# A language-model block chain on one core: RWKV outputs split one round later, two output units projected inside the last round

## The reference

```python
def _rwkv7_scan(r, w, k, v, a, b):
...
    def step(S, inp):
        r_t, w_t, k_t, v_t, a_t, b_t = inp
        sa = jnp.einsum('bhij,bhj->bhi', S, a_t)
        S = (S * w_t[:, :, None, :] + sa[..., None] * b_t[:, :, None, :] + v_t[..., None] * k_t[:, :, None, :])
        y = jnp.einsum('bhij,bhj->bhi', S, r_t)
        return S, y
...
    g = jax.nn.sigmoid(xg @ g1) @ g2
...
    y = _rwkv7_scan(r_h, decay.reshape(B, T, H, N), k_h, v_h, -kk, kk * a_h)
    mu = jnp.mean(y, axis=-1, keepdims=True)
    var = jnp.mean(jnp.square(y - mu), axis=-1, keepdims=True)
    y = (y - mu) * lax.rsqrt(var + GN_EPS)
    y = y * gn_w.reshape(H, N).astype(f32) + gn_b.reshape(H, N).astype(f32)
    y = y + jnp.sum(r_h * k_h * r_k.astype(f32), axis=-1, keepdims=True) * v_h
    y = y.reshape(B, T, D).astype(x.dtype)
    return (y * g) @ w_o
```

## Time and profile before

| | |
|---|---|
| median of 3 runs (lowest to highest) | 2088.23 us (2085.95 to 2088.8) |
| profiled execution: span from first to last instruction | 2084.5 us, 3.7 us under the median |
| profiled execution: time of its own beside the span | not listed apart from the three runs |
| TensorE busy, mean granted clock | 1981.5 us (95%), 0.963 |
| VectorE, ScalarE, GpSimd busy | 1061.3, 778.6, 252.0 us |
| RWKV rounds j = 0 to 7 | from about 862 to 1098 us |
| units 0 and 1 of the output projection | 1099.45 to 1112.36 us |

### The profile page before, as it was taken

How to read it: one execution, slowest core, us unless ns; L and a number is a source line. 1 busy time by engine, 2 the same in 40 slices (tenths; PEclk the granted TensorE clock), 3 DMA queues, 4 the chain that set the end, 5 groups by cost and what they waited for, 6 DMA issues and landing times.

```text
span 2084.5 us, 35297 instructions
## 1 busy us (share of the span) xinstructions
PE 1981.5 (95%) x14503; PEld 1583.9 (76%) x14503; DVE 1061.3 (51%) x1567; ACT 778.6 (37%) x1242; POOL 252.0 (12%) x282
## 2 busy tenths in 40 slices
PE   6999899999999999899979999999989999999997
PEld 5767678888885677777767788888867878888886
DVE  6776775555325654678653644442255564444223
ACT  4333433333222345667534333232245343323221
POOL 1100000000014000322211211110100021111110
PEclk8998999999999999899999999999999999999997
DMA  8544323333332232000003133333222223333321
GB/s 307 162 132 122 91 71 100 91 101 103 111 90 63 61 91 75 6 10 9 5 27 89 53 96 95 100 114 97 82 61 82 81 71 100 92 101 99 111 83 41
DMA packets 311057, 181.09 MB, mean 87 GB/s; under 512 B 16381, under 2 KB 303763, under 8 KB 310932
## 3 DMA queue, kind: packets, MB, share of 16 engines
q1 hardware_dynamic: 305506, 162.29, 26.2%
q0 software_dynamic: 4608, 16.78, 2.5%
q10 hardware_dynamic: 818, 0.21, 0.0%
HBM read 177.16 MB, written 2.10 MB: 86 GB/s over the span
## 4 chain that ended last, share of the span: by engine, by line
PE 85%; DVE 8%; issue 3%; ACT 3%; ACTq 1%; POOL 0%; DVEq 0%; POOLq 0%
PE bank L258 22%; PE bank L260 22%; PE bank L259 22%; PE bank L2207 4%; DVE x L1399 1%; PE bank L2704 1%; PE bank L2698 1%; PE bank L1256 1%; ACT whi L236 1%; PE bank L2805 1%; PE bank L562 1%; PE bank L1258 1%; PE bank L1257 1%; PE bank L1997 1%; DVE wlo L243 1%
## 5 line engine op out<-in xcount | busy, mean ns | idle before, releaser
L243 DVE TENSOR_TENSOR wlo<-raw,whi 128x1024 fp32r<-128x1024 f32 (+1 forms) x254 | 331.0, 1304 | 669.9 <-ACT whi L236 669.8
L236 ACT ACTIVATE whi<-raw 128x1024 fp32r<-128x1024 f32 (+1 forms) x254 | 284.1, 1119 | 669.0 <-PE bank L260 663.7
L258 PE MATMUL bank<-fh_hi,whi 128*128 128x512 f32 x991 | 387.7, 391 | 0.9 <-DVE fh_lo L483 0.5
L259 PE MATMUL bank<-fh_lo,whi 128*128 128x512 f32 x991 | 386.3, 390 | 0.0
L260 PE MATMUL bank<-fh_hi,wlo 128*128 128x512 f32 x991 | 386.2, 390 | 0.0
L258 PEld LDWEIGHTS bank<-fh_hi,whi 128*128 128x128 f32 x991 | 186.4, 188 | 42.3 <-DVE fh_lo L483 1.8
L259 PEld LDWEIGHTS bank<-fh_lo,whi 128*128 128x128 f32 x991 | 186.4, 188 | 39.2 <-issue 0.5
L260 PEld LDWEIGHTS bank<-fh_hi,wlo 128*128 128x128 f32 x991 | 186.4, 188 | 38.6
L258 PE MATMUL bank<-f_hi,whi 128*128 128x512 f32 x528 | 205.7, 390 | 0.0
L260 PE MATMUL bank<-f_hi,wlo 128*128 128x512 f32 x528 | 205.4, 389 | 0.0
L259 PE MATMUL bank<-f_lo,whi 128*128 128x512 f32 x528 | 205.4, 389 | 0.0
(11 more groups left out here) (469 smaller groups left out, 3232.8 us busy)
## 6 DMA issues: line engine op xcount, KB each, us to landing
raw<-in_w_up_dram SPq DMA_DIRECT2D x44, 512.0 KB, 3.7
raw<-in_ffn_w_gate_dram SPq DMA_DIRECT2D x44, 512.0 KB, 3.7
raw<-in_ffn_w_up_dram SPq DMA_DIRECT2D x44, 512.0 KB, 3.7
raw<-in_ffn_w_down_dram SPq DMA_DIRECT2D x32, 704.0 KB, 4.3
late<-in_ada_w_dram POOLq DMA_DIRECT2D x32, 512.0 KB, 4.2
raw<-in_rwkv_w_rkv_dram SPq DMA_DIRECT2D x24, 512.0 KB, 3.4
raw<-in_w_down_dram SPq DMA_DIRECT2D x16, 704.0 KB, 4.2
early<-in_ada_w_dram SPq DMA_DIRECT2D x16, 512.0 KB, 14.4
```

What stands on the lines that cost most here:

```text
L236: act.activation(halves_of(at)[0][:, 0:kts * P], raw_unit(at, kts), ACT.Copy).then_inc(hi_ready, 1)
L243: dve.tensor_tensor(lo[:, 0:kts * P], raw_unit(at, kts), hi[:, 0:kts * P].bitcast(F32), ALU.subtract)\
L258: pe.matmul(dst, hi, rhs_hi(k), start=first and k == 0, stop=False)
L259: pe.matmul(dst, hi, rhs_lo(k), start=False, stop=False)
```

## The change

- The splits: in round j (1 to 7) ScalarE splits y of tile j - 1 behind its copy of G, and VectorE makes the lower half behind state 3. `ys_hi` now lies on the memory of the keys (bonus) and `ys_lo` on that of the values, whose tile j - 1 nobody reads any more. After the rounds only tile 7 is split.
- The last round of TensorE is written out (`pe_last_round`): between the steps of the run it makes the products of output units 0 and 1 with tiles 0 to 6, 14 of their 16 products. `Project.pe` only adds tile 7 to both.
- The gate of round 7 goes into bank 4 (RUN_BANK[0]) in two halves, the first behind state 2, the second behind the last output; VectorE's last multiplication waits for a semaphore of its own.
- `o_tm` is placed over memory that the rounds no longer need by then, and the lower halves of the FFN's held weights lie in the last tiles of `f_lo`, since `f_hi`'s tiles now overlap `ys_hi`.

```diff
+                if held_apart:
+                    held[4:] = [self.f_lo[:, n:n + 2, :].rearrange("p a n -> p (a n)") for n in range(KF - 8, KF, 2)]
...
+    with ExitStack() as part:
+        sbs(part, "y_all", [P, KD, T])
+        ys_hi = sbs(part, "ys_hi", [P, KD, T], F32R)
+        ys_lo = sbs(part, "ys_lo", [P, KD, T], F32R)
     rkv = sbs(tm, "rkv", [P, 3 * KD, T])
+    with ExitStack() as part:
+        o_tm = sbs(part, "o_tm", [P, KD, T])
...
+    def gate_bank(j):
+        return POST_BANK if j < KD - 1 else RUN_BANK[0]
...
+    def act_split_y(act, j):
+        DVEc.wait(act, j, "y")
+        act.activation(ys_hi[:, j, :], rkv[:, j, :], ACT.Copy).then_inc(ys_hi_ready, 1)
...
                 act_gt(act, j)
+                if j:
+                    act_split_y(act, j - 1)
...
     def dve_post_gate(dve, j):
-        PEc.wait(dve, j, "g")
+        if j < KD - 1:
+            PEc.wait(dve, j, "g")
+        else:
+            dve.wait_ge(last_gate, 1)
         DVEc.wait(dve, j, "yb")
-        DVEc.done(dve.tensor_tensor(r_k_v(j)[0], y_sb[:, :], bank[POST_BANK][:, :], ALU.mult), "y")
+        DVEc.done(dve.tensor_tensor(r_k_v(j)[0], y_sb[:, :], bank[gate_bank(j)][:, :], ALU.mult), "y")
+    def dve_split_y(dve, j):
+        dve.wait_ge(ys_hi_ready, j + 1)
+        dve.tensor_tensor(ys_lo[:, j, :], rkv[:, j, :], ys_hi[:, j, :].bitcast(F32), ALU.subtract)\
+           .then_inc(ys_ready, 1)
...
                 dve_state(dve, j, 3)
+                if j:
+                    dve_split_y(dve, j - 1)
...
+    def pe_last_gate(pe, part):
+        b = bank[gate_bank(KD - 1)][:, :]
+        if part == 0:
+            wait(pe, lg_landed, KD * 32)
+            ACTr.wait(pe, KD - 1, "gt0")
+            DVEr.wait(pe, KD - 1, "hp1")
+            pe.matmul(b, lg[:, 0, :], g_hid[:, :], start=True, stop=False)
+        else:
+            pe.matmul(b, lg[0:G_REST, 1, :], g_hid2[:, :], start=False, stop=True).then_inc(last_gate, 1)
+    def pe_last_round(pe):
+        j = KD - 1
+        def project(o, *ks):
+            for k in ks:
+                out_tm.pe_early(pe, o, k)
+        pe_xau(pe, j)
+        project(0, 0, 1)
+        pe_state_parts(pe, j)
+        pe_rh(pe, j, None)
+        project(0, 2)
+        pe_state(pe, j, 1)
+        pe_state(pe, j, 2)
+        pe_last_gate(pe, 0)
+        pe_state(pe, j, 3)
+        pe_local(pe, j)
+        pe_state(pe, j, 4)
+        project(0, 3)
+        pe_state(pe, j, 5)
+        project(0, 4)
+        pe_state(pe, j, 6)
+        for c in (6, 1, 3, 5, 4, 2):
+            pe_y(pe, j, c)
+        pe_y(pe, j, 7)
+        pe_last_gate(pe, 1)
+        project(0, 5)
+        pe_post_var(pe, j, None)
+        project(1, 0, 1)
+        pe_post_spread(pe, j)
+        project(1, 2, 3, 4, 5)
+        project(0, 6)
+        project(1, 6)
...
+            if j == KD - 1:
+                pe_last_round(pe)
+                return
...
+        def pe_early(self, pe, o, k):
+            self.y_split(pe, k)
+            unit_products(pe, self.at0.plus(o), KD, bank[o][:, :], lambda k: self.hi[:, k, :],
+                          lambda k: self.lo[:, k, :], True, True, ks=[k])
...
-            wait(pe, o_ready.sem, self.o0)
-            two_units(pe, [self.at0.plus(o) for o in range(2)], KD, [bank[o][:, :] for o in range(2)], hi, lo,
-                      lambda k: self.y_split(pe, k))
+            if self.early:
+                for o in range(2):
+                    self.pe_early(pe, o, KD - 1)
+            else:
+                wait(pe, o_ready.sem, self.o0)
+                two_units(pe, [self.at0.plus(o) for o in range(2)], KD, [bank[o][:, :] for o in range(2)], hi, lo,
+                          lambda k: self.y_split(pe, k))
...
-    def act_split_y(act):
-        DVEc.wait(act, KD - 1, "y")
-        for k in range(KD):
-            act.activation(ys_hi[:, k, :], rkv[:, k, :], ACT.Copy).then_inc(ys_hi_ready.sem, 1)
-    def dve_split_y(dve):
-        DVEc.wait(dve, KD - 1, "y")
-        for k in range(KD):
-            dve.wait_ge(ys_hi_ready.sem, yhi0 + k + 1)
-            dve.tensor_tensor(ys_lo[:, k, :], rkv[:, k, :], ys_hi[:, k, :].bitcast(F32), ALU.subtract)\
-               .then_inc(ys_ready.sem, 1)
...
+    ffn1 = FFN("1", out_tm.end, out_tm.res, gains_of(2), None, wg2[0], wu2[0], wd2[0], False, gains_of(3),
+               held_apart=True)
```

More of the change, by code:

```diff
@@ L1431, in build, with __init__ @@
     class FFN:
-        def __init__(self, tag, at0, before, gains, shift, w_gate, w_up, w_down, conv, out_gains, final=False):
+        def __init__(self, tag, at0, before, gains, shift, w_gate, w_up, w_down, conv, out_gains, final=False,
+                     held_apart=False):
             self.at0, self.conv, self.final = at0, conv, final
@@ L2070, in build @@
     bm.close()
+    ys_hi_ready, ys_ready, last_gate = sem("ys_hi_ready"), sem("ys_ready"), sem("last_gate")
     class Steps:
@@ L3016, in pe_first, with __init__ @@
             pe_low(pe, 1)
-    ys_hi_ready, ys_ready = count("ys_hi_ready"), count("ys_ready")
     class Project:
-        def __init__(self, mem, at0, w, hi, lo, y_split, gains):
-            self.at0, self.w, self.hi, self.lo, self.y_split = at0, w, hi, lo, y_split
+        def __init__(self, mem, at0, w, hi, lo, y_split, gains, early=False):
+            self.at0, self.w, self.hi, self.lo, self.y_split, self.early = at0, w, hi, lo, y_split, early
             self.end = at0.plus(KD)
@@ L3083, in build @@
     gains_of = lambda n: (lambda k: v("gains", n * KD + k))
[L3084 to L3087, removed]
     out_tm = Project(o_tm, at_rkv0.plus(3 * KD), A["rwkv_w_o_2"].rearrange("a k n -> (a k) n"), ys_hi, ys_lo,
-                     lambda eng, k: eng.wait_ge(ys_ready.sem, y0 + k + 1), gains_of(1))
+                     lambda eng, k: eng.wait_ge(ys_ready, k + 1), gains_of(1), early=True)
     tm.close()
-    def act_split_y(act):
-        DVEc.wait(act, KD - 1, "y")
-        for k in range(KD):
-            act.activation(ys_hi[:, k, :], rkv[:, k, :], ACT.Copy).then_inc(ys_hi_ready.sem, 1)
-    def dve_split_y(dve):
-        DVEc.wait(dve, KD - 1, "y")
-        for k in range(KD):
-            dve.wait_ge(ys_hi_ready.sem, yhi0 + k + 1)
-            dve.tensor_tensor(ys_lo[:, k, :], rkv[:, k, :], ys_hi[:, k, :].bitcast(F32), ALU.subtract)\
-               .then_inc(ys_ready.sem, 1)
     wg2, wu2, wd2 = A["ffn_w_gate_2"], A["ffn_w_up_2"], A["ffn_w_down_2"]
-    ffn1 = FFN("1", out_tm.end, out_tm.res, gains_of(2), None, wg2[0], wu2[0], wd2[0], False, gains_of(3))
+    ffn1 = FFN("1", out_tm.end, out_tm.res, gains_of(2), None, wg2[0], wu2[0], wd2[0], False, gains_of(3),
+               held_apart=True)
     out_tm.after = ffn1.first[0:2], ffn1.first[2:4]
@@ L3466, in _ @@
         act_blocks(act)
-        act_split_y(act)
+        act_split_y(act, KD - 1)
         out_tm.act(act)
@@ L3480, in _ @@
         dve_blocks(dve)
-        dve_split_y(dve)
+        dve_split_y(dve, KD - 1)
         out_tm.dve(dve)
```

## The result

The change took 2070.68 us in the median of 4 runs (2070.2 to 2070.95), the kernel before 2087.09 us beside it (2084.59 to 2088.8): a ratio of 0.993, 95% interval 0.9912 to 0.9948. That is 16.4 us off, where 9.5 was forecast, and under the low end of the range, 2074.0.

The account below looks back on a forecast made before the run. TensorE, busy 95% of the span, was taken as the bound, so time is won where it stands or runs slowly. Last round -12.2 and splits +2.7 gave -9.5 us: 2088.2 to 2078.7 us, 8-in-10 range 2074.0 to 2087.5.

Parts of the forecast that it names:

- The tail: Projection behind the last split, up to unit 2's first matmul: 12.9 us becomes 3.4, a gain of 9.5 us.
- the gate: Round 7: with its own bank and both halves early, VectorE's 3.44 us wait before the last y goes; gain 3.4.
- the wait for unit 2's weights: Projection: 2.53 us from ScalarE's start on unit 2's split to its first matmul, counted within the remaining 3.4 us.
- -12.2: Last round and projection in us: tail -9.5, gate -3.4, clock -0.45, fillers +1.15.
- The fillers: Round 7: products of units 0 and 1 and gate halves placed in the chain's holes lengthen it by 1.15 us.
- 0.45 us for the clock: Round 7: with TensorE fed, the clock stays up and the transposes take 0.66 us, not 1.11; gain 0.45.
- The holes in front of Z: VectorE's split delays level 2's Z, opening TensorE holes: 1.1 us each in rounds 2 and 3, 0.5 in round 6.
- So rounds 1, 4 and 5 cost nothing ... they should fall in the same places: Existing TensorE instruction waits at Z,XT recur there beside the late Z, so the split costs 0 in these rounds.
- the rival of the new holes: New holes in rounds 2 or 3 drop the clock, up to 4.2 us each: 2082.9 or 2087.1 us; chance 0.16.
- a clock fall fewer: Part of the reason given, with free splits, for the range's low end of 2074.0 us.
- The 3.7 us around the span: Whole kernel: median of runs lies 3.7 us over the profiled span; carried over from span 2075.0 to 2078.7 us.
- the bounds of the rounds: Rounds 1 to 6: the moved splits cost between 1.7 and 8.5 us, 2.7 taken; stated range 2074 to 2083 us.

Follow-up runs that it names:

- a1: The changed kernel itself, unaltered, timed and profiled again: 2071.9 us, ratio 0.9926 to the kernel before.
- a2: The changed kernel itself, unaltered, timed and profiled once more: 2072.96 us, ratio 0.9933 to the kernel before.
- e8: The changed kernel, with TensorE in round 5 alone made to wait before the products of RH with the states until GpSimd cleared a tile three times: 2073.25 us.
- f2: The changed kernel with VectorE's half of the split moved behind state 7 in every round but round 5: 2073.69 us.
- f1: The kernel before, with VectorE clearing an unused tile five times ahead of Z in round 5 alone: 2083.13 us, ratio 0.9972.
- e9: The changed kernel, with the forced TensorE wait before the products of RH with the states in round 3 alone: 2075.49 us.
- e7: The kernel before, unaltered, timed and profiled again: 2086.53 us.

## Why the prediction was wrong, and where it was right

**What was missed.** The forecast was 2078.7 us, the measured median 2070.68, 8.0 less. By the two profiles on record, measured less forecast is -5.2 in rounds 0 to 6 (-4.1 of them in round 5), +2.4 in the last round, -1.2 ahead of the rounds, -1.8 behind unit 2, and -2.2 outside the profiled span.

**The last round: right in its terms, in its size partly by luck.** The tail, the gate and the wait for unit 2's weights came as worked out. But -12.2 was worked out from the profile on record, where the round took 35.1 us, and so meant 22.9; the change took 25.3 there, with a clock that fell, and 23.7 in `a1` and `a2` at full clock. The fillers cost more: ScalarE's copy of y starts 11.39 us behind XAU, 10.09 before, so 1.3 us later where some 0.6 was worked out up to there (0.05 + 0.35 + 0.2). The mean difference is -12.3 only because the two other profiles of before took 37.2 and 37.3 us: the granted clock over the round was 0.81 on record and 0.73 and 0.72 in these, 0.93 and twice 1.00 in the change. Two windows of 20 us (PE's busy time, PEclk, DMA share, GB/s), before on record and `a2`, show both the holes that were filled and the clock:

```profile
1080.00:1100.00 20.00, 11.55 (x205) 0.74 0.10 29
```

```profile
1080.00:1100.00 20.00, 18.05 (x173) 1.00 0.11 32
```

So the forecast's 0.45 us for the clock was too small. That the gate's 3.4 us is half bank and half clock was not seen either. The fillers' terms add to 1.2 us, not 1.15, which changes nothing.

**The holes in front of Z: right in kind and size.** 1.1 us was taken; in round 3 the split starts at 960.84 us, E takes 1.22 us and Z starts 8.50 us behind XAU (962.93 - 954.43), where it was 7.35: 1.15 us later, and TensorE waits 1.16.

```profile
960.84 1.03 DVE L2614 TENSOR_TENSOR ys_lo<-rkv,ys_hi 128x512 fp32r<-128x512 f32 x1
961.79 1.22 DVE L2473 TENSOR_TENSOR E_t<-L_t,tmp 128x512 f32<-128x512 f32 x1
962.93 0.74 DVE L2548 TENSOR_TENSOR Z<-bank,eye 128x256 f32<-128x256 f32 x2
963.73 0.56 PEld L2221 LDWEIGHTS bank<-Z,XT 64*64 64x64 f32 x32 [1.29 <-DVE Z L2548]
963.73 0.69 PE L2221 MATMUL bank<-Z,XT 64*64 64x64 f32 x32 [1.16 <-DVE Z L2548]
```

By the exclusion rule of the Trainium skill, "SBUF — State Buffer", section "Who interferes with whom", the prediction estimated 1.3; the measured 1.15 is nearer to the row of E. Rounds 2 and 3, taken at 1.1 each, lost 0.95 and 0.5 us in the mean, and round 6, taken at 0.5, nothing. (A split is 4.27/8 = 0.53 us of ScalarE and not 0.6, which enters no sum.)

**The step that failed: "So rounds 1, 4 and 5 cost nothing ... they should fall in the same places".** For rounds 1 and 4 it held: no change in the mean. In round 5 the forecast read the earlier trace rows right, as waits for instructions, and then took them for fixed. It followed only the stall of 1.08 us within Z,XT, on which the new hole lies, and not the stall of 0.79 us 4.85 us behind it, which has no row there. That second one is 256 instructions later. With the hole ahead of it the code packet mostly comes 1.1 us behind the start of Z,XT in place of 2.3, the stall is gone, and with it the 10 us at half clock that the earlier trace rows already showed: round 5 took 5.0 us less in the mean where nothing was forecast. The prediction priced such a fall at up to 4.2 us, as a danger in rounds 2 and 3 (the rival of the new holes). That the change could take an existing one away it did not work out: the low end of its range has "a clock fall fewer", with no mechanism, and at 2.0 us in place of 4.2. At its own price that end would have been 2071.8. That the stall brings the long round is shown by `e8`, in one profile. That the hole takes the stall away is shown in part: without it none of five profiles is free of the stall, with it eight of eleven are (`e8` left out, where a hole was forced); `f2` is a hit, and `f1` a miss whose hole left a stop of 0.20 us. What makes the code come that little too late in spite of a hole stays open.

**The 3.7 us around the span: wrong.** The profiled execution of the kernel after has a span of 2069.2 us and a time of 2070.89 us, and in every other run the two differ by 1.7 or 1.8 us. The rest, 2.0 us, was the distance of one execution of before from its median; the profiled execution of the kernel after lies 0.2 us above its own. So only the 1.7 us carried over, and 2.0 us of the 8.0 is that guess. The prediction's own range was off too: the bounds of the rounds, 1.7 to 8.5 us, give 2077.7 to 2084.5 us, not 2074 to 2083.

**The rest,** -1.1 us ahead of the rounds and -1.7 behind unit 2, was not forecast and not tried. The first stretch is the same code in both kernels and varies by 3 us between executions of one kernel.

## What to carry to other kernels

Where TensorE runs at the edge of its instruction supply with many small matmuls, as in round 5 here, a wait in one place can go together with the loss of a stall in another, and the stall's price need not be its length: 0.87 us cost 5.4 with the clock that fell behind it. Before a hole is costed as a loss, look for stalls released by "issue" that follow it, count the instructions between them, and look at what the clock does behind them. And cut the span into stretches in several executions before a median is explained by a part.

## What the runs showed that was not expected

- The stalls released by "issue" in round 5 stand 256 instructions apart in eight traces (127 matmuls, 127 weight loads, two semaphore instructions), and end 2.4 to 2.8 us behind a packet of instructions of 0.02 MB.
- Whether the second stall came went with a stop of 0.17 us or more in the middle of Z,XT, 127 matmuls ahead of it: it came in eight of the nine profiles that have the stop, and by itself in none of the eight that have not.
- Holes of the same length cost 1.1 us in round 3 (`e9`) and 5.4 us in round 5 (`e8`), where the clock fell to 1.2 GHz for some 10 us.
- Unchanged code on one core spreads over 12 us (`e7`: 2080.56 to 2092.95), and in three profiles of it the last round took 35.1, 37.3 and 37.2 us with a granted clock of 0.81, 0.73 and 0.72.
